# The router's chunks of a decoder step on two column halves of the array, and ranks counted in bfloat16

## The chip, the core and the metric

One core of a Trainium2 chip runs the whole program. It has a matrix engine (TensorE, in the profile PE, with its weight loads apart as PEld), a vector engine (VectorE, DVE), ScalarE (ACT), GpSimd (POOL) and a queue engine for transfers (SyncE, SP), all of them reading one on-chip memory (SBUF) of 128 partitions; TensorE writes to PSUM, eight banks of 512 f32 values in each partition. The metric is the time of one execution on the device, in microseconds; several executions are timed and their median is taken.

## The reference

One layer of a hybrid decoder over 1024 prompt rows and 8 sample rows, width 1024, all in f32. Two token mixers (sparse attention and a gated spatial one) give `merged`. What matters here comes behind them:

```
h = layer_norm(alpha * x + merged @ w_o, ln1_g, ln1_b)
lg = h @ w_router_group + b_router_group          # 4 groups
gsel = argmax(lg)
le = h @ w_router_expert[gsel] + b_router_expert  # 8 experts in each group
vals, eidx = top_k(le, 2)
weights = softmax(vals) * softmax(lg)[gsel]
f = sum over the two experts of  weight * (silu(h @ w_gate) * (h @ w_up)) @ w_down
y = layer_norm(alpha * h + f, ln2_g, ln2_b)
```

The kernel works only on the rows that chose an expert. So each row needs its two experts and, for each of them, its rank: how many rows ahead of it chose the same expert. The rank gives the row's place in the expert's list.

## The kernel before

The program runs through stages, each a block with an instruction list for every engine: projections and scores, choice of keys and gates, attention, then `merge_route_and_experts`, which the change touches. Engines signal one another by semaphores (`then_inc` and `wait_ge`); each list is worked off in the order in which it is written, and that order is set by hand.

**Merge.** 24 units, each the second branch's product of one block of 128 columns with a third of the rows (L1634 on TensorE), which VectorE multiplies with a gate and adds to (L1778, L1781). `gates` has three buffers. VectorE opens the block with a few clears (L1769 to L1772). Behind unit 16 (`FOLD_AT`) it folds the layer norm's gain into the router's weights, `w_fold` (L1786); TensorE later sums these over all rows (L1705).

**Projection and routing.** Nine tiles of 128 rows; the first has only 8 rows in use and is projected in another way (L1643). `project(i)` for i from 1 to 8 has 16 matmuls of 128x512 (two column halves c, eight chunks k, L1663), and between them stand the steps for the tile before, i - 1:

- ahead of matmul 2 (`TURN_AT`): `turn`, eight 128x128 transposes of h (L1675), which ScalarE copies to `hT` (L1754);
- ahead of 4 (`ROUTE_AT`): `route`, eight matmuls (L1685). The folded weights (128x36, a chunk of the width each) are stationary, `hT` (128x128) moves, and all eight add up to the logits of 4 groups and 32 experts, 36 partitions x 128 rows in PSUM;
- ScalarE copies these to `lgT` (L1759);
- ahead of 6 (`LOGITS_AT`): `turn_logits`, a transpose of `lgT` to 128 rows x 36 (L1691), which VectorE reads (L1900);
- VectorE chooses (`pick`): `both` is 1 where a row chose an expert, `chosen` the running count by row (L1818, L1824). Then it finishes h (L1930);
- ahead of 12 (`RANK_AT`): `rank`, two matmuls of 128x32 into one result: `earlier` (a triangle of ones) with `both` (L1699), and `ones` with `chosen` (L1700). VectorE turns the ranks into places (`place`, L1831 to L1847).

On VectorE the additions of the next tile (L1892, one for each column half) and their statistics (L1872) stand around `place`.

**Behind the ninth tile.** TensorE has `turn`, `route`, the sum of the first list of tokens (L1716), `turn_logits`, `rank`. VectorE makes `first_tokens` of that sum (L1869), GpSimd gathers these rows of h (L1970), and TensorE puts the first expert's rows together (L1724, L1731). The end of `route` also lets SyncE issue the load of the fourth expert's weights (L1582). Then come the 24 packs of the expert stage (L2087, L2100, L2119), whose weights have four buffers that are filled as the work goes on.

`ones` is f32, and so are `earlier`, `both` and `chosen`. `ident` is the 128x128 identity.

Of the kernel before, what the change touches and what calls it, by code (L numbers as in the profile page):

```python
# [12 lines left out]
F32 = mybir.dt.float32  # L13
BF16 = mybir.dt.bfloat16
# [6 lines left out]
P = 128  # L21
D = 1024
KC = D // P
# [3 lines left out]
TILES = NT + 1  # L27
# [1380 lines left out]
N_EXPERTS = 32  # L1408
# [10 lines left out]
SLOTS = TOK * N_EXPERTS  # L1419
NOWHERE = float(1 << 20)  # L1420
ROUTER = N_GROUPS + N_EXPERTS


def merge_route_and_experts(nc, ins, outs, keep, scratch):

    with nc.cleanup_on_exit(), ExitStack() as ctx:
        def sb(name, shape, dt=F32):
            return ctx.enter_context(nc.sbuf_tensor(name, shape, dt))
# [4 lines left out]
        ident, attnT, logits = keep["ident"], keep["attnT"], keep["router_logits"]  # L1433
        best_g, best1, best2 = (keep["best"][:, n, :] for n in range(3))
        chosen = keep["chosen"]
# [10 lines left out]
        w_fold = mergedT[:, :, SEQ + 32:SEQ + 32 + 2 * ROUTER].rearrange("p k (a r) -> p k a r", a=2)  # L1446
        h = keep["h_rows"]

        over = attnT[:].rearrange("p k n -> p (k n)")
        hT = over[:, 0:D].rearrange("p (k n) -> p k n", k=KC)  # L1450
# [12 lines left out]
        valid, away = sb("valid", [P, TILES]), sb("away", [P, TILES])  # L1463
        entry = sb("entry", [P, 2, TILES], U32)
        earlier = sb("earlier", [P, P])
        off_group = sb("off_group", [P, N_GROUPS])
        marked, rest, waste = (over[:, D + n * N_EXPERTS:D + (n + 1) * N_EXPERTS] for n in range(3))
        highest = sb("highest", [P, 1])
        lgT = over[0:ROUTER, D + 3 * N_EXPERTS:D + 3 * N_EXPERTS + P]
        FREE = D + 3 * N_EXPERTS + P  # L1470
        free = [over[:, FREE + n * N_EXPERTS:FREE + (n + 1) * N_EXPERTS] for n in range(10)]
        choice = [free[2 * n:2 * n + 2] for n in range(2)]
        both = free[4:6]
        after = FREE + 10 * N_EXPERTS + 2 * ROUTER
        e4 = over[:, after:after + TILES * N_GROUPS].rearrange("p (t g) -> p t g", g=N_GROUPS)
        e2, sum_g, den = (over[:, after + TILES * (N_GROUPS + n):after + TILES * (N_GROUPS + n + 1)] for n in range(3))
# [6 lines left out]
        ps = keep["ps"]  # L1483

        w_o_in, w_r_in, const_in = sem("w_o_in"), sem("w_r_in"), sem("m_const_in")
        fold_ready, folded, fold_read = sem("fold_ready"), sem("folded"), sem("fold_read")
# [18 lines left out]
        ranked = sem("ranked")  # L1505
# [122 lines left out]
        def _(pe):  # L1628
# [49 lines left out]
            def route(i):  # L1678
                pe.wait_ge(hT_read, 2 * i + 2)
                if i == 0:  # L1680
                    pe.wait_ge(fold_read, 2)
                else:
                    pe.wait_ge(logits_read, i)
                for k in range(KC):
                    mm = nc.tensor.matmul(ps[0:ROUTER, ROUTED, 0:P], w_fold[:, k, 0, :], hT[:, k, :],  # L1685
                                          start=(k == 0), stop=(k == KC - 1))
                mm.then_inc(routed, 1)

            def turn_logits(i):
                pe.wait_ge(lgT_read, i + 1)  # L1690
                nc.tensor.transpose(ps[:, ROUTED, P:P + ROUTER], lgT, ident[0:ROUTER, 0:ROUTER]).then_inc(lg_turned, 1)  # L1691

            def rank(i):

                pe.wait_ge(picked, i + 1)
                if i >= 1:
                    pe.wait_ge(slots_ready, i)
                to = ps[:, RANKS, 0:N_EXPERTS]
                nc.tensor.matmul(to, earlier[:], both[i % 2], start=True, stop=False)  # L1699
                nc.tensor.matmul(to, ones[:], chosen[:, i, :], start=False, stop=True).then_inc(ranked, 1)  # L1700

            pe.wait_ge(rows_zeroed, 1)
            pe.wait_ge(fold_ready, 2)
            for k in range(KC):
                mm = nc.tensor.matmul(ps[:, ROUTED, FOLD0:FOLD0 + 2 * ROUTER], ones[:],  # L1705
                                      w_fold[:, k, :, :].rearrange("p a r -> p (a r)"), start=(k == 0), stop=(k == KC - 1))
# [34 lines left out]
            rank(TILES - 1)  # L1741
            assemble_first()
            sum_tokens(1)
            nc.tensor.matmul(ps[:, TURNED[1], 0:N_EXPERTS], ones[:], chosen[:, TILES, :], start=True, stop=True).then_inc(counted, 1)
            main.tensor(pe)

        @block.scalar
        def _(act):
            for t in range(TILES):
                for c in range(2):  # L1750
                    act.wait_ge(h_turned, 2 * t + c + 1)
                    if t >= 1:
                        act.wait_ge(routed, t)
                    nc.scalar.copy(hT[:, c * 4:(c + 1) * 4, :],  # L1754
                                   ps[:, 6 + c, :].rearrange("p (k q) -> p k q", q=P)).then_inc(hT_read, 1)
                act.wait_ge(routed, t + 1)
                if t >= 1:
                    act.wait_ge(lg_turned, t)
                nc.scalar.copy(lgT, ps[0:ROUTER, 2, 0:P]).then_inc(lgT_read, 1)  # L1759
            main.scalar_first(act)  # L1760
            act.wait_ge(exp_ready, 2)
            nc.scalar.activation(e4, e4, ACT.Exp).then_inc(exped, 1)
            nc.scalar.activation(e2, e2, ACT.Exp).then_inc(exped, 1)
            main.scalar(act)

        @block.vector
        def _(dve):
            step = Chain(dve, dve_step)
            step(nc.vector.memset(chosen[:, 0, :], 0.0), wait=False)  # L1769
            step(nc.vector.memset(ones[:], 1.0), wait=False)  # L1770

            nc.vector.memset(mergedT[:, :, SEQ + N_SAMPLE:SEQ + FEW], 0.0).then_inc(rows_zeroed, 1)  # L1772
            for n, (blk, p) in enumerate(units):
                c0, width = PIECES[p]
                to = mergedT[:, blk, c0:c0 + width]
                dve.wait_ge(branch, n + 1)
                dve.wait_ge(gates_in[n % 3], 32 * (n // 3 + 1))
                nc.vector.tensor_tensor(to, ps[:, FIRST_BANK + n % 3, 0:width], gates[n % 3][:, 0, 0:width],  # L1778
                                        ALU.mult).then_inc(merged, 1)
                dve.wait_ge(merged, 2 * n + 1)  # L1780
                nc.vector.tensor_tensor(to, to, gates[n % 3][:, 1, 0:width], ALU.add).then_inc(merged, 1)  # L1781
                if n == FOLD_AT:
                    dve.wait_ge(w_r_in, 16)
                    dve.wait_ge(const_in, 16 * N_CONST)
                    for which in range(2):
                        nc.vector.tensor_tensor(w_fold[:, :, which, :], w_r[:],  # L1786
                                                ln1_t[:, which, :].unsqueeze(2).to_broadcast([P, KC, ROUTER]),
                                                ALU.mult).then_inc(fold_ready, 1)
            dve.wait_ge(folded, 1)
            nc.vector.tensor_scalar(minus_sum, ps[:, ROUTED, FOLD0:FOLD0 + ROUTER], -1.0, None, ALU.mult).then_inc(fold_read, 1)  # L1790
            nc.vector.tensor_tensor(b_r[:], b_r[:], ps[:, ROUTED, FOLD0 + ROUTER:FOLD0 + 2 * ROUTER], ALU.add).then_inc(fold_read, 1)
# [664 lines left out]
def build(nc, ins, outs, scratch):  # L2456
    with ExitStack() as whole:
        def sb(name, shape, dt=F32, side="left", ctx=whole):
            return ctx.enter_context(nc.sbuf_tensor(name, shape, dt, side=side))
# [35 lines left out]
        keep["w_gu_in"], keep["w_dn_in"] = ([whole.enter_context(nc.semaphore(f"{n}_expert{j}")) for j in range(W_BUFS)]  # L2495
                                            for n in ("w_gu_in", "w_dn_in"))
        for name, shape, dt in (("router_logits", [P, TILES, ROUTER], F32), ("weights", [P, 2, TILES], F32),
                                ("best", [P, 3, TILES], F32), ("chosen", [P, TILES + 1, N_EXPERTS], F32), ("ones", [P, P], F32),
                                ("h_rows", [P, TILES, D], F32), ("entries", [P, N_EXPERTS], U32), ("tokens", [P, N_EXPERTS], U32), ("most", [1, 1], I32)):
            keep[name] = sb(name, shape, dt)  # L2500
        keep["w_o"] = sb("w_o", [P, KC, D])
# [105 lines left out]
```

## Time and profile before

| | us |
|---|---|
| median of 3 runs | 1419.87 |
| the three runs | 1413.06, 1419.87, 1420.9 |
| span of the profiled execution | 1417.2 |
| PE busy | 1351.4 (95%) |
| PEld busy | 695.7 (49%) |
| DVE busy | 716.3 (51%) |
| ACT busy | 281.6 (20%) |
| POOL busy | 241.0 (17%) |
| DMA | 214.14 MB, mean 151 GB/s |

The profile is one execution, from its first to its last instruction. Times of its rows are counted from the span's start. The stage that the change touches lies between 845 and 1072 us. An f32 matmul shows as two records on PE and two on PEld, a transpose and a bfloat16 matmul as one. A row's duration covers the record's way through the array, so records that follow one another overlap; what one costs in a stream is the distance from its start to the next start. Numbers such as 128*36 in a row are rows and columns of the array in use.

### The profile page before, as it was taken

How to read it: one execution, taken by the hardware profiler on the slowest of the kernel's cores; microseconds unless marked ns; L12 is line 12 of the kernel's file. 1: busy time of each engine (PE TensorE's matmuls, PEld its weight loads, DVE VectorE, ACT ScalarE, POOL GpSimd, SP SyncE). 2: the span in 40 equal slices, each digit the busy share in tenths (PEclk: the TensorE clock that was granted, in tenths of full speed). 3: DMA queues.
4: the chain of work that ended last, by engine and by line, in shares of the span. 5: the costliest groups of instructions: out<-in, count | busy, mean ns of one | idle time of the engine just before them, and what ended most of it. 6: DMA issues, size and time to landing. Idle time of an engine off the chain costs nothing. (4 is left out here: it accounts for less than half of the span.)

```text
span 1417.2 us, 19227 instructions
## 1 busy us (share of the span) xinstructions
PE 1351.4 (95%) x6699; PEld 695.7 (49%) x6699; DVE 716.3 (51%) x1700; ACT 281.6 (20%) x624; POOL 241.0 (17%) x292
## 2 busy tenths in 40 slices
PE   8999999899999999999899989999988999999995
PEld 2444444344456666666577655555544333333321
DVE  0211123388888888997265853577782111111126
ACT  0100122232231111111266430000001111111115
POOL 3122000034330000011034400011111111111113
PEclk9999999999999999999899999999998999999998
DMA  9311002220022111110032319921135899999936
GB/s 323 94 51 60 17 16 75 76 65 0 0 101 73 68 67 67 67 67 31 26 101 66 127 43 332 366 103 30 30 102 231 329 399 410 405 408 413 407 140 259
DMA packets 70316, 214.14 MB, mean 151 GB/s; under 512 B 16059, under 2 KB 41915, under 8 KB 59866
## 3 DMA queue, kind: packets, MB, share of 16 engines
q1 hardware_dynamic: 56266, 184.74, 34.7%
q0 software_dynamic: 12688, 27.76, 5.8%
q8 instruction: 53, 0.87, 0.2%
q10 hardware_dynamic: 1280, 0.53, 0.2%
q14 instruction: 29, 0.24, 0.1%
HBM read 186.47 MB, written 34.65 MB: 156 GB/s over the span
## 5 line engine op out<-in xcount | busy, mean ns | idle before, releaser
L259 PE MATMUL ps_mixer<-front,x_all 128*128 128x512 f32 (+1 forms) x448 | 180.4, 557 | 1.7 <-ACT wi L407 1.7
L953 DVE TENSOR_SCALAR_CACHE_REDUCE front<-score,bound 128x384 bf16<-128x384 f32 (+2 forms) x198 | 174.0, 940 | 0.4 <-DVE bound L975 0.3
L259 PEld LDWEIGHTS ps_mixer<-front,x_all 128*128 128x128 f32 x448 | 83.2, 190 | 91.7 <-issue 81.2
L1663 PE MATMUL ps<-w_o,mergedT 128*128 128x512 f32 x256 | 117.7, 602 | 0.0
L2087 PE MATMUL ps<-w_gate_up,w_o 128*32 128x512 f32 (+1 forms) x640 | 113.2, 594 | 1.5 <-DVE w_o L2171 1.5
L781 PE MATMUL ps_mixer<-x_all,front 128*128 128x344 f32 x384 | 114.4, 453 | 0.0
L781 PE MATMUL ps_mixer<-x_all,w_gate 128*128 128x344 f32 x384 | 113.3, 453 | 0.0
L2087 PE MATMUL ps<-w_a,w_o 128*64 128x512 f32 (+1 forms) x256 | 113.1, 594 | 0.0
L2196 DVE TENSOR_TENSOR w_o<-w_o,ps 128x256 f32<-128x256 f32 x24 | 10.1, 420 | 164.0 <-ACT w_o L2151 164.0
L781 PEld LDWEIGHTS ps_mixer<-x_all,w_gate 128*128 128x128 f32 x384 | 72.7, 190 | 37.5
L781 PEld LDWEIGHTS ps_mixer<-x_all,front 128*128 128x128 f32 x384 | 72.6, 190 | 37.1
L953 DVE TENSOR_SCALAR_CACHE_REDUCE front<-score_s,bound 8x2049 bf16<-8x2049 f32 x33 | 77.0, 2334 | 0.0
L1663 PEld LDWEIGHTS ps<-w_o,mergedT 128*128 128x128 f32 x256 | 46.0, 190 | 48.2 <-issue 47.8
L2087 PEld LDWEIGHTS ps<-w_gate_up,w_o 128*32 128x32 f32 (+1 forms) x640 | 33.1, 115 | 68.8 <-issue 68.8
L935 POOL TENSOR_TENSOR front<-front 128x344 f32<-128x344 f32 x24 | 25.2, 1048 | 243.7 <-ACT front L895 243.7
L2065 POOL DMA_INDIRECT pair_out<-w_o,entries x24 | 25.0, 1042 | 236.1 <-DVE w_o L2203 236.1
L892 ACT ACTIVATE front<-ps_mixer,gate_bias 128x344 f32<-128x344 f32 x48 | 26.2, 547 | 175.8 <-PE ps_mixer L781 175.7
L1634 PE MATMUL ps<-attnT,w_a 128*128 128x344 f32 x186 | 56.0, 464 | 4.4 <-DVE mergedT L1778 2.9
L2119 PE MATMUL ps<-w_down,w_o 128*32 128x512 f32 (+1 forms) x320 | 60.0, 619 | 0.0
L2119 PE MATMUL ps<-gates,w_o 128*32 128x512 f32 (+1 forms) x128 | 58.1, 597 | 0.5 <-ACT w_o L2156 0.5
L729 PE MATMUL ps_mixer<-front,x_all 128*128 128x512 f32 x128 | 57.4, 592 | 0.0
L2087 PE MATMUL ps<-mergedT,w_o 128*32 128x512 f32 x384 | 56.5, 594 | 0.0
(342 smaller groups left out, 1933.6 us busy)
## 6 DMA issues: line engine op xcount, KB each, us to landing
w_gate_up<-in_w_gate_up SPq DMA_DIRECT2D x16, 2048.0 KB, 15.2
w_down<-in_w_down SPq DMA_DIRECT2D x16, 1024.0 KB, 16.6
w_a<-in_w_gate_up SPq DMA_DIRECT2D x8, 2048.0 KB, 11.7
mergedT<-in_w_gate_up SPq DMA_DIRECT2D x8, 2048.0 KB, 16.9
gates<-in_w_down SPq DMA_DIRECT2D x8, 1024.0 KB, 7.9
mergedT<-in_w_down SPq DMA_DIRECT2D x8, 1024.0 KB, 10.4
front<-in_w_qkvi SPq DMA_DIRECT2D x7, 930.0 KB, 16.7
w_gate<-in_w_gate SPq DMA_DIRECT2D x4, 1280.0 KB, 6.2
```

Of the source, the lines that this page charges most:

```text
L259: mm = nc.tensor.matmul(ps[:, g % 2, 0:c1 - c0], x_all[:, k, t * P:(t + 1) * P], w[:, k, c0:c1], start=(k == 0), stop=(k == KC - 1))
L729: mm = nc.tensor.matmul(ps[:, bank, :], x_all[:, k, t * P:(t + 1) * P], w_uv(k)[:, half * GW:(half + 1) * GW], start=(k == 0), stop=(k == ...
L781: mm = nc.tensor.matmul(ps[:, SETS[at % 2][which], 0:n], w_gate[j][:, which * KC + k, :], right[:, k, c0:c0 + n], start=(k == 0), stop=(k ...
L892: op = nc.scalar.activation(to, src, ACT.Sigmoid, bias=gate_bias[:, which, bass.ds(i * 2 + j, 1)])
L935: nc.gpsimd.tensor_tensor(m[:, 1, 0:n], m[:, 1, 0:n], m[:, 2, 0:n], ALU.mult).then_inc(multiplied, 1)
L953: V.tensor_scalar(waste[0:n, at - width:at], s, column(bound, g), None, compare, ALU.add, accum_out=column(number, g)).then_inc(taken, 1)
L1634: mm = nc.tensor.matmul(ps[:, FIRST_BANK + n % 3, 0:width], w_a[:, k, blk * P:(blk + 1) * P], attnT[:, k, c0:c0 + width], start=(k == 0), ...
L1663: mm = nc.tensor.matmul(ps[:, PROJECTED[i % 2][c], :], mergedT[:, k, t * P:(t + 1) * P], w_o[:, k, c * 512:(c + 1) * 512], start=(k == 0), ...
L2065: pool.indirect_dma_start(out=scratch["pair_out"].rearrange("t w q j d -> (t w q j) d"), out_offset=bass.IndirectOffsetOnAxis(ap=entries[: ...
L2087: mm = nc.tensor.matmul(ps[c0:c1, GU, :], rowsT[j][:, k, c0:c1], w_gu[b][:, k, :], start=(k == 0), stop=(k == KC - 1))
L2119: mm = nc.tensor.matmul(ps[c0:c1, 4 + 2 * j + c, :], hiddenT[j][:, k, c0:c1], w_dn[b][:, k, c * 512:(c + 1) * 512], start=(k == 0), stop=( ...
L2196: nc.vector.tensor_tensor(hidden[j], hidden[j], ps[:, GU, F:2 * F], ALU.mult).then_inc(hid, 1)
```

## The change

The router's even chunks go to the array's columns from 0 on, the odd ones to those from 64 on, and so to PSUM partitions 0 to 35 and 64 to 99: two sums of four chunks. ScalarE copies 100 partitions. The turn is no longer a transpose but an f32 matmul with `stack`, 100 rows x 36, which holds the identity in rows 0 to 35 and again in rows 64 to 99, so that it turns and adds the halves at once. Partitions between the halves are cleared once. For the ranks, `both` and `chosen` are written in bfloat16, `ones_b` and `earlier_b` are bfloat16 copies of the two stationary tiles, and the count of all rows (L1744) uses them too.

```diff
+LG_ROWS = P // 2 + ROUTER
...
+        earlier_b, ones_b = sb("earlier_b", [P, P], BF16), sb("ones_b", [P, P], BF16)
+        stack = sb("stack", [P, ROUTER])
...
-        lgT = over[0:ROUTER, D + 3 * N_EXPERTS:D + 3 * N_EXPERTS + P]
+        lgT = over[0:LG_ROWS, D + 3 * N_EXPERTS:D + 3 * N_EXPERTS + P]
...
-        both = free[4:6]
+        both = [free[4 + n].bitcast(BF16)[:, 0:N_EXPERTS] for n in range(2)]
...
                 for k in range(KC):
-                    mm = nc.tensor.matmul(ps[0:ROUTER, ROUTED, 0:P], w_fold[:, k, 0, :], hT[:, k, :],
-                                          start=(k == 0), stop=(k == KC - 1))
+                    half = k % 2 * (P // 2)
+                    mm = nc.tensor.matmul(ps[half:half + ROUTER, ROUTED, 0:P], w_fold[:, k, 0, :], hT[:, k, :],
+                                          start=(k < 2), stop=(k >= KC - 2))
...
-                nc.tensor.transpose(ps[:, ROUTED, P:P + ROUTER], lgT, ident[0:ROUTER, 0:ROUTER]).then_inc(lg_turned, 1)
+                nc.tensor.matmul(ps[:, ROUTED, P:P + ROUTER], lgT, stack[0:LG_ROWS, :], start=True, stop=True).then_inc(lg_turned, 1)
...
-                nc.tensor.matmul(to, earlier[:], both[i % 2], start=True, stop=False)
-                nc.tensor.matmul(to, ones[:], chosen[:, i, :], start=False, stop=True).then_inc(ranked, 1)
+                nc.tensor.matmul(to, earlier_b[:], both[i % 2], start=True, stop=False)
+                nc.tensor.matmul(to, ones_b[:], chosen[:, i, :], start=False, stop=True).then_inc(ranked, 1)
...
-            pe.wait_ge(fold_ready, 2)
+            pe.wait_ge(fold_ready, 3)
...
-                nc.scalar.copy(lgT, ps[0:ROUTER, 2, 0:P]).then_inc(lgT_read, 1)
+                nc.scalar.copy(lgT, ps[0:LG_ROWS, ROUTED, 0:P]).then_inc(lgT_read, 1)
...
+            step(nc.vector.memset(ones_b[:], 1.0), wait=False)
+            step(nc.vector.memset(ps[P // 4:P // 2, ROUTED, 0:P], 0.0), wait=False)
+            step(nc.vector.memset(stack[:], 0.0))
+            for q0 in (0, P // 2):
+                step(nc.vector.tensor_copy(stack[q0:q0 + ROUTER, :], ident[q0:q0 + ROUTER, q0:q0 + ROUTER]), wait=False)
...
+                    nc.vector.tensor_copy(earlier_b[:], earlier[:]).then_inc(fold_ready, 1)
...
-                                ("best", [P, 3, TILES], F32), ("chosen", [P, TILES + 1, N_EXPERTS], F32), ("ones", [P, P], F32),
+                                ("best", [P, 3, TILES], F32), ("chosen", [P, TILES + 1, N_EXPERTS], BF16), ("ones", [P, P], F32),
```

## Rows read from the trace of the kernel before

**Rows 1.** Stretches: bounds, length, busy by engine (x instructions), PEclk, DMA share, GB/s.

```profile
947.08:964.58 17.50, 17.50 (x63) 9.00 (x62) 12.88 (x45) 1.33 (x3) 2.66 (x4) 1.00 0.12 30
1066.00:1067.00 1.00, 1.00 (x7) 1.00 (x6) 0.85 (x3) 0.00 (x0) 0.00 (x0) 0.50 0.00 0
1143.00:1359.00 216.00, 216.00 (x1624) 73.46 (x1624) 32.43 (x54) 34.66 (x72) 34.45 (x34) 1.00 0.94 386
```

**Rows 2.** TensorE's timeline, one tile: start us, us, engine, line, out<-in, xcount.

```profile
947.08 1.04 PE L1675 MATMUL ps<-ident,h_rows 128*128 128x128 f32 x8
947.95 1.88 PE L1663 MATMUL ps<-w_o,mergedT 128*128 128x512 f32 x4
949.76 1.94 PE L1685 MATMUL ps<-attnT,mergedT 128*36 128x128 f32 x16
951.63 1.98 PE L1663 MATMUL ps<-w_o,mergedT 128*128 128x512 f32 x4
953.55 0.25 PE L1691 MATMUL ps<-ident,attnT 36*128 36x36 f32 x1
953.73 5.42 PE L1663 MATMUL ps<-w_o,mergedT 128*128 128x512 f32 x12
958.98 0.30 PE L1699 MATMUL ps<-attnT,earlier 128*128 128x32 f32 x2
959.12 0.39 PE L1700 MATMUL ps<-chosen,ones 128*128 128x32 f32 x2
959.34 5.40 PE L1663 MATMUL ps<-w_o,mergedT 128*128 128x512 f32 x12
```

**Rows 3.** The same tile on ScalarE and VectorE; in brackets idle time before.

```profile
951.74 0.26 ACT L1759 COPY attnT<-ps 36x128 f32<-36x128 f32 x1 [2.95 <-PE ps L1685]
...
953.91 0.25 DVE L1900 SCALAR_TENSOR_TENSOR attnT<-attnT,mv,ps 128x36 f32<-128x36 f32 x1 [3.40 <-PE ps L1691]
...
963.12 0.69 DVE L1892 SCALAR_TENSOR_TENSOR h_rows<-h_rows,ps 128x512 f32<-128x512 f32 x1
```

**Rows 4.** The timeline behind the ninth tile, VectorE, SyncE's queue and TensorE.

```profile
1053.90 1.28 DVE L1922 SCALAR_TENSOR_TENSOR h_rows<-h_rows,mv,ln 128x1024 f32<-128x1024 f32 x1
...
1054.77 0.33 SPq L1582 DMA_DIRECT2D mergedT<-in_w_gate_up  x1
...
1055.11 0.15 DVE L1869 TENSOR_SCALAR first_tokens<-ps 128x1 uint32<-128x1 f32 x1
...
1059.85 0.41 PE L1699 MATMUL ps<-attnT,earlier 128*128 128x32 f32 x2 [2.60 <-DVE attnT L1818]
...
1060.10 0.39 PE L1700 MATMUL ps<-chosen,ones 128*128 128x32 f32 x2
```

**Rows 5.** From the chain that ended last: start us, us, what.

```profile
1056.07 8.01 DMA w_o<-h,first_tokens
```

**Rows 6.** TensorE's timeline in the attention stage, two column halves of 64.

```profile
727.14 1.04 PE L1207 MATMUL ps<-ident,total 128*64 128x128 f32 x16
728.12 0.33 PE L1181 MATMUL ps<-ident,probs 128*128 128x128 f32 x1
```

**Rows 7.** TensorE's timeline, the single projection records ahead of turn and rank.

```profile
953.02 0.59 PE L1663 MATMUL ps<-w_o,mergedT 128*128 128x512 f32 x1
...
958.55 0.59 PE L1663 MATMUL ps<-w_o,mergedT 128*128 128x512 f32 x1
```

**Rows 8.** TensorE's timeline, bfloat16 matmuls among f32 ones in the gate stage.

```profile
651.91 0.55 PE L807 MATMUL ps_mixer<-ids_by_half,front 128*128 128x4 bf16 x16
652.32 4.87 PE L781 MATMUL ps_mixer<-x_all,front 128*128 128x344 f32 x16
```

**Rows 9.** VectorE's timeline, the first unit of the merge and the one after the fold.

```profile
847.97 0.52 DVE L1778 TENSOR_TENSOR mergedT<-ps,gates 128x344 f32<-128x344 f32 x1 [2.30 <-DMA gates<-merged_b]
...
891.65 0.52 DVE L1778 TENSOR_TENSOR mergedT<-ps,gates 128x344 f32<-128x344 f32 x1 [0.40 <-DMA gates<-merged_b]
```

**Rows 10.** The router's line: duration ns min/median/max, first and last start, forms.

```profile
L1685 PE MATMUL ps<-attnT,mergedT x144: 272/273/301, 914.8 to 1054.5; 128*36 128x128 f32 x144
```

More of the change, by code:

```diff
@@ L1743, in _ @@
             sum_tokens(1)
-            nc.tensor.matmul(ps[:, TURNED[1], 0:N_EXPERTS], ones[:], chosen[:, TILES, :], start=True, stop=True).then_inc(counted, 1)
+            nc.tensor.matmul(ps[:, TURNED[1], 0:N_EXPERTS], ones_b[:], chosen[:, TILES, :], start=True, stop=True).then_inc(counted, 1)
             main.tensor(pe)
```

## Prediction

> **What bounds the kernel now.** I read the table of stretches first, then the chain of waits, then the timelines of single engines inside one tile. In a tile of the routed projection TensorE is busy for all 17.50 us at full granted clock, with DMA at a share of 0.12 [rows 1]: TensorE's instruction order sets the pace, and each microsecond taken out of it is a microsecond of the span as long as no other engine becomes the last one. The 17.50 us are: eight transposes 0.87, four projection records 1.81, the router's 16 records 1.87 (949.76 to 951.63), four projection records 1.92, the turn of the logits 0.18, twelve records 5.25, the rank's four records 0.36 (958.98 to 959.34), twelve records 5.24 [rows 2]. An f32 matmul leaves two records, an f32 transpose one. The change touches only the 1.87, the 0.18 and the 0.36. Eight such tiles stand one behind the other, and the ninth's router stands in the tail.
>
> VectorE waits once in a tile, 3.40 us for the turned logits; from there (953.91) it works without a gap to the second half of the next addition (963.12) [rows 3]. Behind the ninth tile the chain leaves TensorE: VectorE runs to the first token list (1055.11) [rows 4], then a gather of 8.01 us holds everything [rows 5]. The expert stage is TensorE again, 216.00 us of 216.00 busy, with DMA at 0.94 beside it [rows 1].
>
> **The router on two column halves.** Removed: eight matmuls one after the other, 16 records at 1.87 / 16 = 0.117 us. Added: the same 16 records, alternating between columns 0 and 64 of the array. The nearest row has the same shape (128x128 moving, 64-column tiles, two halves alternating, also 16 records): L1207 starts at 727.14 and the next group at 728.12, so 0.98 us, 0.061 a record [rows 6]. Saved: 1.87 - 0.98 = 0.89 a tile. Ends: 0.053 a record (a 512-wide f32 record takes 0.43 [rows 7], a quarter of it is 0.107, and half of that) gives 1.02 saved; no overlap at all gives nothing. I take 0.89, because that row agrees in shape, type, count and order.
>
> The Trainium skill speaks against this. Its page "TensorE: Matmul & The Clock Gate" (Part 3, The mechanism) says that weight loads overlap matmuls in flight only when the row group differs, and both halves here use all rows. By it the halves would gain nothing and the sum would be that of rival A; the 0.061 of L1207, where the row groups don't differ either, disagrees.
>
> **The turn of the logits.** Removed: a transpose of one record on 36 rows. It costs 0.18 itself, and the projection record ahead of it lasts 953.55 - 953.02 = 0.53, against 0.43 for the record ahead of the rank (958.55 to 958.98) [rows 2, 7]: 0.10 more, paid where the array goes from 128 rows to 36. Together 0.28. Added: an f32 matmul with 100 rows and 36 columns moving, two records. The nearest is the rank's first matmul (128 rows, 32 moving), two records in 0.14 with its first weight load hidden [rows 2]. 100 rows need the whole array, so the 0.10 should go too. I take 0.14, saving 0.14. The other end: nothing hidden, 0.25 as in the tail (1059.85 to 1060.10) [rows 4], and still the 0.10: a loss of 0.07 a tile. For VectorE the second record comes about 0.03 later, so its wait ends 0.07 earlier, not 0.14.
>
> The Trainium skill, "TensorEngine Tiling (Array Packing)", Tiling Modes, says that a change of tiling mode drains the engine and a change of tile doesn't. The trace agrees in both parts (0.53 against 0.43, and L1207's cheap alternation). Were the 0.10 no drain but kept, the sum would be 0.7 us smaller.
>
> **The rank in bfloat16.** Removed: four f32 records, 0.36. Added: two bf16 records. Row: 16 bf16 records of L807 from 651.91 to 652.32, 0.026 each, among f32 matmuls and with no pause ahead of them [rows 8]. Two make 0.05; saved 0.31. The other end is half of the present price, 0.18 saved. I take 0.31, since L807 has the same 128x128 bf16 weights. Values are zeros, ones and counts to nine.
>
> **What is hidden.** At the block's start VectorE gets two more clears, one of a PSUM quadrant, one of the stack, and two 36-column copies: five small instructions. At 0.25 each, what L1900 takes on 36 columns [rows 3], that is 1.3 us; the first product waits 2.30 us for its gates anyway [rows 9]. Queued behind them are the zeroing of the merged rows, whose signal TensorE needs only after all 24 units, and nothing else early. The cast of the triangle comes behind unit 16, ahead of a wait of 0.40 [rows 9]; a product of 344 columns takes 0.52 [rows 9], so some 0.2 for 128 columns is my estimate and fits; if not, it delays one product by a few tenths, with three buffers of slack ahead of TensorE. No DMA is added or moved. ScalarE copies 100 partitions in place of 36; its copy (0.26) ends at 952.00, the turn begins at 953.55 [rows 2, 3], so even at five times the time it would be covered. VectorE writes its choices in bf16 with the same number of instructions; twelve projection records cover them, as now. If the cover of the start were gone it would be 1.3 us.
>
> **Who is late next.** A tile becomes 17.50 - 0.89 - 0.14 - 0.31 = 16.16 us. VectorE's loop: from the first transpose (947.08) to the start of L1900 (953.91) 6.83, after the change 6.83 - 0.89 - 0.07 = 5.87; then 9.21 without a gap to L1892 and its 0.69 [rows 2, 3]: 15.77. Only the second four transposes wait for it, 0.43 into their group, so with a signal of under 0.1 VectorE allows a tile each 15.4 us. TensorE at 16.16 stays the last, with some 0.7 to spare.
>
> **The sum.** The tail hangs on VectorE from the eighth turn (tile 7) on, so what counts is how much earlier that one comes: eight routers 8 x 0.89 = 7.12; seven turns 7 x 0.14 and the eighth's 0.07, 1.05; seven ranks 7 x 0.31 = 2.17. Together 10.34 us. The ninth tile's own router isn't last: the first token list follows VectorE's L1922 directly (1053.90 + 1.28, then 1055.11 [rows 4]). But its end releases the fourth expert's weights (issue at 1054.77), which share the DMA engines with the gather of 8.01 us [rows 4, 5]. They start 0.89 earlier against the gather: between 0 and 0.89 back, I take 0.5. Sum 10.8 us. The profiled execution's span is 1417.2 and becomes 1406.4. The median of the runs, 1419.87, is 2.7 above the span, with the same work around it: **1409.0 us**. With the other ends of turn and rank it is 7.12 - 0.49 + 1.26 = 7.9, 1412.0; with the best ends 8 x 1.02 + 1.05 + 2.17 + 0.89 = 12.3, 1407.6. The three runs before spread over 7.8 us, so a median is good to about 3.
>
> **Rivals.**
> A. The halves don't overlap: a record on one half waits for the other's, 0.117 each as now. Left are turn and rank, 3.2 us: **1416.7**. For it only that this kernel's router tiles are 36 wide, not 64; against it L1207. Chance 0.07.
> B. The front gain is given back behind the ninth tile. TensorE ran the assembly there at a granted clock of 0.50 (1.2 of 2.4 GHz), after it had idled for the gather [rows 1]. With less work around the idle time it may fall earlier or rise later and take the first expert products along: 7 us of these at half clock would cost 7. The expert stage's DMA share of 0.94 also leaves gathers little room, so that a changed meeting with a weight load may cost 1 to 4. Against: no transfer there runs by its own clock; the loads are released by TensorE's progress and move along. I price it at 3.5 lost: **1412.5**. Chance 0.16.
> C. Slower: each change of half drains. A record lasts 0.273 [rows 10]; if each of the router's eight changes waited for that, it would take 16 x 0.117 + 8 x 0.273 = 4.06, 2.19 more, less 0.45 for turn and rank: 1.74 a tile, 14 us, **1434**. It decides from a price of 0.17 a change (0.98 + 8 x 0.17 = 1.87 + 0.45). The drain seen is 0.10, at changes of mode only. Chance 0.03.
> D. The change is compiled to something else (a 36-column tile placed at 64 taking the whole array, say): within 0.3% of before. Chance 0.04, near **1418**.
>
> **How the numbers follow.** Forecast 0.70 at 1409.0, its own range 1406 to 1413. The range for 8 in 10 reaches to B and to the edge of A: 1405 to 1417. Over or under 0.5%, about what a measurement of this kernel can tell from no change, means under 1412.8: nine tenths of the forecast's 0.70 and half of B, 0.71. Slower by 0.5% is C and chance, 0.04. The rest, 0.25, is A, D, half of B and the edge of the forecast.
>
> **What would show it.** Right: the router's 16 records in 0.95 to 1.0 us; the projection record ahead of the turn at 0.43; two bf16 records in under 0.1; a tile period near 16.2; VectorE's wait at L1900 down from 3.40 to about 2.1; first token list some 10 us earlier than 1055.11; an expert stage of the same length. Wrong: router records still at 0.117 (A), or longer (C); a period at 15.4 or above 16.5 with TensorE waiting for VectorE's additions; an assembly and first expert that take 3 us more (B).

## The result and the profile after

| | before | after |
|---|---|---|
| median of the runs timed together, us | 1419.05 (4 runs) | 1406.53 (4 runs, 1406.22 to 1408.59) |
| ratio after / before, 95% | | 0.9916, 0.9896 to 0.9936 |
| span of the profiled execution, us | 1417.2 | 1407.2 |
| one tile of the routed projection, us | 17.50 | 16.17 |
| router / turn / rank on TensorE, us | 1.87 / 0.18 / 0.36 | 1.00 / 0.14 / 0.06 |
| first token list written, us | 1055.11 | 1045.37 |

Timed once more with six runs, the changed kernel came to 1405.24 us, ratio 0.9912 (0.9896 to 0.9927). It is 0.8 to 0.9% faster.

The table of stretches of the changed kernel, with the columns of [rows 1]: a tile, and the expert stage.

```profile
945.00:961.17 16.17, 16.17 (x61) 7.90 (x60) 12.88 (x45) 1.34 (x3) 2.66 (x4) 1.00 0.13 33
1142.00:1347.00 205.00, 205.00 (x1546) 69.82 (x1538) 30.68 (x51) 32.73 (x68) 32.42 (x32) 1.00 0.95 388
```

TensorE is still busy for the whole tile, and VectorE has the same 12.88 us of work in it as before. TensorE's order sets the pace as it did; the tile is simply 1.33 us shorter. The expert stage looks as it did in [rows 1].

TensorE's timeline of that tile, which answers to [rows 2]:

```profile
945.00 1.04 PE L1678 MATMUL ps<-ident,h_rows 128*128 128x128 f32 x8
945.87 1.88 PE L1666 MATMUL ps<-w_o,mergedT 128*128 128x512 f32 x4
947.69 1.07 PE L1689 MATMUL ps<-attnT,mergedT 128*36 128x128 f32 x16
948.69 1.98 PE L1666 MATMUL ps<-w_o,mergedT 128*128 128x512 f32 x4
950.51 0.31 PE L1695 MATMUL ps<-stack,attnT 100*128 100x36 f32 x2
950.65 5.40 PE L1666 MATMUL ps<-w_o,mergedT 128*128 128x512 f32 x12
955.88 0.18 PE L1703 MATMUL ps<-attnT,earlier_b 128*128 128x32 bf16 x1
955.91 0.18 PE L1704 MATMUL ps<-chosen,ones_b 128*128 128x32 bf16 x1
955.94 5.40 PE L1666 MATMUL ps<-w_o,mergedT 128*128 128x512 f32 x12
```

As before, the differences of starts are what one reads, not the durations, since pipelined records overlap. The router's 16 records take 948.69 - 947.69 = 1.00 us, the turn's two 0.14, the rank's two 0.06. The weight loads of the same stretch show two more things:

```profile
947.68 0.81 PEld L1689 LDWEIGHTS ps<-attnT,mergedT 128*36 128x36 f32 x16 [0.76 <-issue]
...
950.08 0.19 PEld L1695 LDWEIGHTS ps<-stack,attnT 100*128 100x128 f32 x1 [0.24 <-issue]
```

The first load of the turn runs at 950.08, under the last projection record, which takes 0.43 us (950.08 to 950.51) where [rows 7] had 0.53. The router's first load does not run ahead: it starts at 947.68, together with its matmul (947.69). The four projection records in front of it take 1.82 us (945.87 to 947.69) in place of four times 0.43, so about 0.10 us is paid there, as it was before the change.

ScalarE and VectorE of the tile, with idle time before in brackets, which answers to [rows 3]; the last row is VectorE's first product of the merge, which answers to [rows 9]:

```profile
948.80 0.27 ACT L1763 COPY attnT<-ps 100x128 f32<-100x128 f32 x1 [2.09 <-PE ps L1689]
...
950.94 0.25 DVE L1909 SCALAR_TENSOR_TENSOR attnT<-attnT,mv,ps 128x36 f32<-128x36 f32 x1 [2.07 <-PE ps L1695]
...
960.14 0.69 DVE L1901 SCALAR_TENSOR_TENSOR h_rows<-h_rows,ps 128x512 f32<-128x512 f32 x1
```

```profile
848.63 0.52 DVE L1786 TENSOR_TENSOR mergedT<-ps,gates 128x344 f32<-128x344 f32 x1 [1.32 <-DMA gates<-merged_b]
```

VectorE's wait fell from 3.40 to 2.07 us, and the 9.20 us behind it (950.94 to 960.14) are the old 9.21. At the front, the first product still waits for its gates, 1.32 us where it was 2.30: the new small instructions took 0.98 us out of a wait.

SyncE's issue of the fourth expert's weights and VectorE's first token list, then the chain that ended last behind the ninth tile, which answer to [rows 4, 5]:

```profile
1044.17 0.33 SPq L1585 DMA_DIRECT2D mergedT<-in_w_gate_up  x1
...
1045.37 0.15 DVE L1878 TENSOR_SCALAR first_tokens<-ps 128x1 uint32<-128x1 f32 x1
```

```profile
1046.33 7.77 DMA w_o<-h,first_tokens
1054.24 3.75 PE ps L1728 x16
...
1064.42 2.30 DMA list_of<-entry,slot_out
...
1069.99 11.94 DMA w_o<-h,tokens
...
1083.07 5.27 PE ps L2128 x32
```

The chain is the old one. The gather of the first token rows takes 7.77 us where it took 8.01.

To compare runs I cut every profiled execution at the same events. The columns, in us: the merge stage's first gates load (a time); from there to the first record of the few-row projection; on to VectorE's read of the eighth turned logits; on to the issue of the first token gather; on to the first expert product; on to the transposes of the third pack; on to those of the fourth; on to the end.

```
                       start   few  8th read gather product pack3 pack4    end    span
before                845.16 60.55   135.70  14.66  15.88  19.94 13.66 311.65  1417.2
after                 845.75 60.54   125.49  14.55  15.76  19.88 13.67 311.56  1407.2
after_again           844.90 60.41   125.49  14.55  14.84  19.99 11.96 310.56  1402.7
e1_halves_only        847.50 59.76   127.67  14.56  14.43  20.18 11.97 310.23  1406.3
e2_ranks_only         845.45 62.75   133.52  14.54  15.88  20.01 13.60 311.45  1417.2
e3_turn_only          845.32 58.86   134.60  14.56  16.46  20.10 11.97 310.63  1412.5
e4_halves_in_blocks   845.94 61.25   129.20  14.54  14.42  19.61 13.60 311.54  1410.1
e9_halves_in_pairs    848.70 62.56   125.70  14.56  14.03  19.52 13.60 311.63  1410.3
e6_late_load          845.66 60.80   125.49  14.55  12.67  21.46 11.96 311.41  1404.0
e7_early_list         844.49 60.25   125.49  14.55  14.81  19.49 11.97 310.45  1401.5
e8_both               847.98 62.40   125.49  14.55  12.88  18.81 13.47 310.82  1406.4
e10_early_list_calm   845.39 59.85   125.49  14.55  15.08  16.10 11.97 311.57  1400.0
e11_.._late_loads     849.52 62.33   125.50  14.54  12.89  16.10 11.97 311.75  1404.6
```

(In the last row the label is shortened: e11_early_list_late_loads.) Between before and after, the column of the eighth read gives 10.21 us, and all others together 0.2 the other way. In that column programs with the same instructions agree to 0.01 us, while the first two columns scatter by 5 and 4 us. That is why the terms are judged in it, not by the medians.

### The profile page after: what moved, and what is told of

The parts are those of the page before. It is cut to its first block and busy times, and to the rows that moved or that the text cites. A ratio compares the mean times of both kernels' runs of the same rounds, so it can differ in the third digit from the quotient of the medians.

```text
span 1407.2 us, 19213 instructions
## 1 busy us (share of the span) xinstructions
PE 1339.1 (95%) x6689; PEld 684.7 (49%) x6689; DVE 717.5 (51%) x1706; ACT 281.8 (20%) x624; POOL 241.4 (17%) x292
```

## Experiments

### The three edits apart

**The halves without the bfloat16 ranks** (e1). The rank goes back to f32, the rest stays:

```diff
-                nc.tensor.matmul(to, earlier_b[:], both[i % 2], start=True, stop=False)
-                nc.tensor.matmul(to, ones_b[:], chosen[:, i, :], start=False, stop=True).then_inc(ranked, 1)
+                nc.tensor.matmul(to, earlier[:], both[i % 2], start=True, stop=False)
+                nc.tensor.matmul(to, ones[:], chosen[:, i, :], start=False, stop=True).then_inc(ranked, 1)
```

> The halves and the stacked turn, with the ranks back in f32 (no bfloat16 copies). Theory (three separate costs on TensorE's list): router 16 records in 1.00 us as in the changed kernel, turn 0.14, rank back at 0.36 from 0.06, so a tile period of 16.17 + 0.30 = 16.47 us and 8 us gained against before, 1411. Rival (the bfloat16 writes also relieve VectorE, and that is part of the gain): the period is longer than 16.47.

Measured: 1409.13 us (ratio 0.9937, 0.9918 to 0.9956). TensorE's timeline at the rank:

```profile
957.48 0.30 PE L1702 MATMUL ps<-attnT,earlier 128*128 128x32 f32 x2
...
957.84 5.40 PE L1665 MATMUL ps<-w_o,mergedT 128*128 128x512 f32 x12
```

The rank is back at 0.36, router and turn stay at 1.00 and 0.14, and the eighth read comes 2.18 us later than in the changed kernel.

**The ranks alone** (e2): the kernel before with `earlier_b`, `ones_b`, `both` and `chosen` in bfloat16 and nothing else.

> The kernel before with the ranks in bfloat16 alone. Theory: period 17.50 - 0.30 = 17.20 us, 7 to 8 times 0.30 = 2.2 us gained, which timing alone can hardly tell from nothing. Rival (a bfloat16 matmul among f32 ones costs a switch): rank over 0.10 us and a period above 17.3.

Measured: 1417.39 us (0.9994, 0.9976 to 1.0011). TensorE's timeline at the rank:

```profile
960.86 0.18 PE L1700 MATMUL ps<-attnT,earlier_b 128*128 128x32 bf16 x1
960.88 0.18 PE L1701 MATMUL ps<-chosen,ones_b 128*128 128x32 bf16 x1
960.91 5.40 PE L1664 MATMUL ps<-w_o,mergedT 128*128 128x512 f32 x12
```

0.05 us instead of 0.36, and the eighth read 2.18 us earlier than before: seven ranks of 0.31, the same from both sides. By the medians alone, a change of 2 us can't be seen here.

**The turn alone** (e3): ranks in f32, and all eight chunks of the router on columns 0 to 35 again. The stacked turn stays, and the PSUM tile is cleared whole, so that rows 64 to 99 add zeros.

```diff
-                    half = k % 2 * (P // 2)
+                    half = 0
                     mm = nc.tensor.matmul(ps[half:half + ROUTER, ROUTED, 0:P], w_fold[:, k, 0, :], hT[:, k, :],
-                                          start=(k < 2), stop=(k >= KC - 2))
+                                          start=(k == 0), stop=(k == KC - 1))
```

> Ranks in f32, all eight router chunks on columns 0 to 35 as before, but the turn by the 100-row matmul with the stack (the second half is zeros). Theory (the 0.10 ahead of the turn is the price of going from 128 rows to 36): the projection record ahead of the turn lasts 0.43 in place of 0.53, the turn 0.14, router still 1.87, period 17.50 - 0.14 = 17.36, and 1 us gained. Rival (the 0.10 is the price of the wait on the copy, which stays here): 0.53 ahead of the turn and a period of 17.46 or more.

Measured: 1416.71 us (0.9996, 0.9977 to 1.0014). TensorE's timeline:

```profile
947.93 1.94 PE L1688 MATMUL ps<-attnT,mergedT 128*36 128x128 f32 x16
949.80 1.98 PE L1665 MATMUL ps<-w_o,mergedT 128*128 128x512 f32 x4
951.62 0.31 PE L1694 MATMUL ps<-stack,attnT 100*128 100x36 f32 x2
951.76 5.40 PE L1665 MATMUL ps<-w_o,mergedT 128*128 128x512 f32 x12
```

The router is at 1.87 again, so the columns alone make its gain. The four projection records ahead of the turn take 1.82 us (949.80 to 951.62) where they took 1.92, and the turn takes 0.14: 0.14 a tile, and the eighth read is 1.10 us earlier. The 0.10 thus belonged to the 36-row tile, not to the wait in front of it, which is still there. Nor does a transpose as such cost it: in [rows 2] the twelve projection records ahead of the 128-row transposes take 5.24 us (959.34 to 964.58, the end of the tile in [rows 1]), those ahead of the rank 5.25. It goes with what the Trainium skill says in "TensorEngine Tiling (Array Packing)", Tiling Modes, that a change of mode drains the array and a change of tile does not: the 100-row tile needs the whole array, as its neighbours do.

The three parts add up: 2.18 for the ranks, 1.10 for the turn, and 10.21 - 2.18 - 1.10 = 6.93 for the halves, which is 8 x 0.867.

### How the halves overlap

**Chunks 0 to 3 on the first half, 4 to 7 on the second** (e4): one change of half in place of seven.

```diff
-                    half = k % 2 * (P // 2)
+                    half = k // (KC // 2) * (P // 2)
                     mm = nc.tensor.matmul(ps[half:half + ROUTER, ROUTED, 0:P], w_fold[:, k, 0, :], hT[:, k, :],
-                                          start=(k < 2), stop=(k >= KC - 2))
+                                          start=(k % (KC // 2) == 0), stop=(k % (KC // 2) == KC // 2 - 1))
```

> The changed kernel with chunks 0 to 3 on the first half and 4 to 7 on the second, in this order, so the half changes once in a router and not at each chunk. Theory (two halves overlap only where matmuls of both stand next to each other in the list): nearly no overlap, 16 records in 1.87 - 0.06 to 1.87, period 17.0 us, 1413. Rival 1 (shorter sums or 64-column weights are what makes it fast): 1.00 and 16.17 as with alternation. Rival 2 (the array looks ahead through its list far enough to run both halves at once): also near 1.0.

Measured: 1411.42 us (0.9945, 0.9925 to 0.9965). TensorE's timeline:

```profile
949.51 1.53 PE L1689 MATMUL ps<-attnT,mergedT 128*36 128x128 f32 x16
950.98 1.98 PE L1666 MATMUL ps<-w_o,mergedT 128*128 128x512 f32 x4
```

A miss. I had thought that only records that follow each other overlap, so that a block order would cost as much as one half. The router takes 1.47 us, 0.40 less than one half does, and the eighth read comes 3.71 us after that of the alternating order: 8 x 0.46. The starts of the single records in the trace show where the 0.40 comes from. The first five start at 949.51, 949.65, 949.76, 949.87 and 949.98, the 0.11 apart that one half needs. Then a second series begins, at 949.98, 950.12, 950.23 and so on, while the first goes on at 950.08, 950.19 and 950.30. The trace doesn't name a record's half; but each series keeps the 0.11 of one half, so the second can only be the other half, started while three of the first half's eight records were still to start. TensorE looked ahead in its list past these three and took a matmul out of the order in which they were written.

**A change of half every second chunk** (e9):

```diff
-                    half = k % 2 * (P // 2)
+                    half = k // 2 % 2 * (P // 2)
                     mm = nc.tensor.matmul(ps[half:half + ROUTER, ROUTED, 0:P], w_fold[:, k, 0, :], hT[:, k, :],
-                                          start=(k < 2), stop=(k >= KC - 2))
+                                          start=(k in (0, 2)), stop=(k in (5, 7)))
```

> The changed kernel with the half changed at each second chunk (0, 1 on the first, 2, 3 on the second and so on). With alternation the 16 records take 1.00 us, in blocks of four chunks they took 1.47, where 1.87 was the price in one half. Theory, formed after the blocks (a matmul starts as soon as its own half is free, as far as some four records ahead): pairs are four records, so close to full overlap, 1.0 to 1.1 us. Rival (only direct neighbours overlap, one matmul at each change): the blocks saved 0.40 at one change, pairs have three and would save at most what alternation does, but end at 1.2 or more.

TensorE's timeline:

```profile
952.71 1.10 PE L1689 MATMUL ps<-attnT,mergedT 128*36 128x128 f32 x16
953.74 1.98 PE L1666 MATMUL ps<-w_o,mergedT 128*128 128x512 f32 x4
```

1.03 us, and 125.70 against 125.49 for the eighth read. Here two records start 0.01 us apart from the first pair on (952.709 and 952.722), although three more of the first half stand between them in the list. Four records in a row on one half are bridged almost fully, eight aren't. The reading of e4 holds, and the rival that asked for 1.2 us or more falls. The one time of this kernel, 1412.08 us, says nothing on it: the stage ahead began 3 us late and took 2 us longer (848.70 and 62.56 in the table).

### What limits the tile next

**Much less work on TensorE** (e5): the router takes only chunks 0 and 1, and the projection leaves out chunks 3 and 5.

```diff
+                        if k in (3, 5):
+                            continue
...
-                for k in range(KC):
+                for k in (0, 1):
...
-                                          start=(k < 2), stop=(k >= KC - 2))
+                                          start=True, stop=True)
```

> The changed kernel with part of TensorE's work left out, so its outputs are not the reference's: the router adds only chunks 0 and 1 of 8, and each projection half leaves out chunks 3 and 5 of 8. It asks how far VectorE is from being the last in a tile. TensorE's own list would take 16.17 - 0.75 - 8 x 0.43 = 12.0 us a tile. Theory (VectorE's run of 9.9 us without a gap, then second half of the transposes, two projections, router, one projection, turn and read): 9.9 + 0.05 + 0.43 + 1.82 + 0.25 + 0.96 + 0.40 = 13.8 us a tile, with TensorE waiting for VectorE's second addition. Rival (VectorE is no limit as long as its busy share is under 0.8): 12.0.

TensorE's timeline, with what ended its idle time, and VectorE's behind the turned logits:

```profile
951.35 0.19 PE L1705 MATMUL ps<-attnT,earlier_b 128*128 128x32 bf16 x1 [0.82 <-DVE attnT L1829]
...
957.10 0.66 PE L1680 MATMUL ps<-ident,h_rows 128*128 128x128 f32 x4 [0.72 <-DVE h_rows L1903]
...
965.36 0.19 PE L1705 MATMUL ps<-attnT,earlier_b 128*128 128x32 bf16 x1 [0.82 <-DVE attnT L1829]
```

```profile
961.16 0.25 DVE L1911 SCALAR_TENSOR_TENSOR attnT<-attnT,mv,ps 128x36 f32<-128x36 f32 x1
...
970.37 0.69 DVE L1903 SCALAR_TENSOR_TENSOR h_rows<-h_rows,ps 128x512 f32<-128x512 f32 x1
```

The tile takes 14.01 us (951.35 to 965.36), 0.2 above the theory's and 2.0 above the rival's time. (The single run's 1394.59 us isn't compared: with work left out, other rows go to the experts.) TensorE now waits twice in it, 0.72 for VectorE's addition ahead of the second four transposes and 0.82 for the picks ahead of the rank; the second wait was in no expectation. VectorE goes from the turned logits to its addition in the same 9.21 us. So the loop through VectorE is real and as long as the forecast had it, and the changed kernel at 16.17 runs just above it.

### The meeting of loads and gathers behind the ninth tile

The forecast let the fourth expert's load move by 0.89 us against the gather of the first rows. How much that load costs the gather was a guess. Five kernels and the changed kernel again ask for it.

> The changed kernel once more, beside the kernel before and the two variants of this call, to hold their times against. Theory: 10 to 12 us under before.

Measured: 1405.24 us (0.9912, 0.9896 to 0.9927); the gather takes 7.42 us.

**The load behind the last store of h** (e6):

```diff
-                if i + 1 == TILES:
-                    sp.wait_ge(routed, TILES)
-                    sp.dma_start(keep["w_gate_up"][W_AHEAD][:], ins["w_gate_up"][W_AHEAD]).then_inc(keep["w_gu_in"][W_AHEAD], 16)
...
                                  ).then_inc(h_out if i + 1 < TILES else last_h_out, 16)
+            sp.wait_ge(routed, TILES)
+            sp.dma_start(keep["w_gate_up"][W_AHEAD][:], ins["w_gate_up"][W_AHEAD]).then_inc(keep["w_gu_in"][W_AHEAD], 16)
```

> The changed kernel with the fourth expert's weights (2 MB) issued behind the last store of h, no longer ahead of the gather of the first token list. Theory (the gather's 7.8 us are the load's, which shares the DMA engines): the gather takes some 4.6 us, the assembly starts 3 us earlier, and 3 to 5 us are gained against the changed kernel, as the weights are needed only by the third pack. Rival (the load's bytes must pass at some time, and now meet the expert stage's gathers): the gather is shorter, but the stall of TensorE ahead of the second pack's successor (3.0 us) grows by as much; no gain.

Measured: 1404.85 us (0.9901, 0.9887 to 0.9916). From the chain that ended last:

```profile
1046.50 4.45 DMA w_o<-h,first_tokens
...
1061.51 3.62 DMA list_of<-entry,slot_out
...
1068.30 12.29 DMA w_o<-h,tokens
```

The gather falls to 4.45 us, so the load costs it 3.0 to 3.3 by the two profiles of the changed kernel, and the first expert product comes 2.2 to 3.1 us earlier. But the scatter of the token list now meets the load, 3.62 for 2.30, and the third pack takes 21.46 for 19.88 to 19.99: half is given back.

**The last tile's list ahead of the second gather** (e7): GpSimd issues the last two scatters one step earlier.

```diff
+            for which in range(2):
+                scatter(TILES - 1, which)
             pool.wait_ge(first_ready, 2)
             pool.wait_ge(last_h_out, 32)
...
-            for which in range(2):
-                scatter(TILES - 1, which)
```

> The changed kernel with the last tile's two entries scattered on GpSimd ahead of the second first-token gather, in place of behind it. Theory (the list waits only for GpSimd's order): its choices are ready at 1054.3, so the list can be read some 6 us earlier, the gather of the third pack starts at about 1063 in place of 1070, TensorE's stall of 3.0 us before 1082 goes with the low clock after it: 3 to 5 us gained. Rival (the gather lands late because the DMA engines are full, whenever it is issued): no gain.

Measured: 1403.56 us (0.9895, 0.9874 to 0.9916). GpSimd's timeline, and from the chain:

```profile
1053.73 1.06 POOL L1605 DMA_INDIRECT list_of<-entry,slot_out  x1 [7.88 <-DVE slot_out L1856]
...
1059.26 1.07 POOL L1979 DMA_INDIRECT w_o<-h,first_tokens  x1 [3.19 <-DVE first_tokens L1878]
```

```profile
1059.26 9.12 DMA w_o<-h,first_tokens
...
1070.50 8.65 PE ps L2096 x32
```

The wait for the third pack is gone, and another stands in its place: the second gather of first rows, issued at 1059.26, takes 9.12 us among the loads that SyncE issued from 1057.62 on.

**Both** (e8).

> Both moves at once. Theory: the gains add up, 6 to 9 us under the changed kernel, near 1399. Rival: one of them takes the other's room, no more than the better of the two.

Measured: 1405.61 us (0.9908, 0.9891 to 0.9926). From the chain:

```profile
1060.73 6.04 DMA list_of<-entry,slot_out
```

The late load now falls on the scatter, 6.04 us for 2.30. Product (12.88) and third pack (18.81) come earlier than in the changed kernel, but together 2.7 us later than in e11 below, where the load meets neither gather nor scatter: the gains of e6 and e7 don't add.

**The early list with the next loads held back** (e10): as e7, and SyncE waits with the down weights of the fourth expert (index `W_BUFS - 1`, 3; the expectation calls them the third's) and the layer norm rows behind them until the second gather has landed.

```diff
-                sp.wait_ge(rows_in[0], 16)
+                sp.wait_ge(rows_in[1], 16)
                 load_down(W_BUFS - 1)
```

> The variant with the early list, and the third expert loads (1 MB of w_down and 1 MB of layer norm rows) wait for the second first-token gather, not the first. With the early list alone they were issued at 1057.6 to 1059.0, just ahead of that gather (1059.26), which took 9.1 us. Theory: the gather takes some 5 us again, the second pack's transposes don't wait, and 2 to 3 us are gained against the early list alone, near 1401. Rival (the loads now meet the next gather, of the third pack, and that becomes the last one): as the early list alone, 1403.6.

Measured: 1403.53 us (0.9894, 0.9877 to 0.9911). From the chain:

```profile
1060.36 7.07 PE ps L2096 x64
...
1069.44 7.09 PE ps L2096 x32
```

The third pack comes after 16.10 us in place of 19.9: the stall is gone and both groups of products run at full pace.

**The same with the fourth load moved to that point as well** (e11).

> As the calm early list, and the fourth expert's 2 MB are issued at the same late point, so that both first-token gathers have the DMA engines to themselves. Theory: the first gather 4.45 in place of 7.2 to 7.8 us, 3 us more, near 1398. Rival (3 MB of loads then meet the third and fourth pack's gathers, as in the variant with both moves, which ended at 1405.6): 1404 or more.

Measured: 1404.55 us (0.9894, 0.9877 to 0.991). The stretches from the gather on are the shortest of all, 12.89 and 16.10. Its profiled execution began the stage 4 us later than e10's (849.52) and took 62.33 to the few rows, for which no run gives a reason.

The times of these variants fell short of what was expected. Against the changed kernel's 1405.24, e6 was to gain 3 to 5 us and gained 0.4; e7 was to gain as much and gained 1.7; e8 was to end near 1399, e10 near 1401, e11 near 1398, and they ended at 1405.61, 1403.53 and 1404.55, as their rivals had it. The stretches show that the waits moved or went; the medians show little of it.

From the few rows to the fourth pack (the sum of five columns) the changed kernel takes 189.35 and 186.83 us in its two profiles, e10 183.19, e11 181.00: 4 to 8 us better. (1.7 us of the distance to the first profile is the clock in the last of these columns, see the last section.) By their medians they are 1 to 3 us better, with intervals that overlap. Both beat the kernel before, by 1.06%; that they beat the changed one isn't shown.

## Why the prediction held, point by point

- **TensorE's order sets the pace.** Right: 16.17 us of 16.17 busy, for a forecast period of 16.16.
- **Router.** 0.87 a tile for the 0.89 taken from L1207 [rows 6]: 6.93 for 7.12. The row of the same shape, type, count and order was the right one to trust. Rival A falls: both halves use all 128 rows, and their records overlap, 1.00 us for 16 against 1.87 on one half in e3. With it falls, for this case, the sentence of the Trainium skill that the forecast set against itself ("TensorE: Matmul & The Clock Gate", Part 3, The mechanism), that weight loads overlap matmuls in flight only when the row group differs. That the halves would then gain nothing was more than the page says: the same Part 3 lists a measured speedup of 2.38 for three tiles packed by columns. Rival C falls too, as no change of half cost anything.
- **Turn.** 0.14 and the 0.10 of drain gone: 1.10 for 1.05 in the sum. e3 shows it by itself.
- **Rank.** 0.31 a tile, 2.18 for 2.17, from both sides in e1 and e2.
- **Hidden work.** The forecast named two clears and two copies and counted five; it is three clears (`ones_b` as well) and two copies, and they took 0.98 us for the 1.3 allowed. The merge's first product still waits 1.32 us for its gates; ScalarE's copy of 100 partitions takes 0.27 for 0.26. VectorE's wait fell to 2.07, forecast about 2.1.
- **Who is late next.** The VectorE loop lies under 16.17, shown with e5. Whether its limit is the 15.4 of the forecast was tested only at 14, where it was 0.2 off.
- **Load against gather.** 0.5 us taken. The two main profiles give 0.24 (8.01 to 7.77) and the second of the changed kernel 0.59 (7.42), but one pair can't size this term. The load was issued 2.16 us ahead of the gather's start (1044.17 to 1046.33) where it had been 1.30, as forecast. Six profiles have the 2.16 (e9 2.14): 7.77, 7.42, e1 7.18, e9 7.18, e7 7.18, e10 6.89, on average 7.27. Three have 1.3: 8.01, e2 8.28, e3 8.13, on average 8.14. That is 0.87, near the upper end of the forecast's 0 to 0.89, and e4 lies between with 1.70 and 7.59. What the forecast didn't see is how much is there: the meeting costs 2.4 to 3.3 us in these six (against 4.45 in e6). In e8 and e11, which move the load too, TensorE starts its assembly 4.47 and 4.53 us behind the gather's issue, in e6 4.58.
- **Rival B** (the gain given back behind the ninth tile) didn't come: product 15.76 for 15.88, third pack 19.88 for 19.94, fourth 13.67 for 13.66. Its mechanisms are real, though: loads and gathers cost each other microseconds in e6 to e8, and the clock does fall there (below).
- **The sum.** 10.3 us earlier at the first token list: 1055.11 - 1045.37 = 9.74, with the stage begun 0.59 later. The profiled spans differ by 10.0. The medians differ by 12.5 and, in the second comparison, 13.4, with intervals of 9.1 to 14.8 and 10.4 to 14.8 us. The 10.21 of the stretch and the 0.87 of the gather's average are 11.1, inside both. The 1.4 to 2.3 us above it aren't located, and with such intervals need not be there. By the ratios of the variants nothing of the kind shows: e1 8.9 us for 8.0 + 0.87 by the trace, e2 0.9 for 2.2, e3 0.6 for 1.1. One thing of this size is on record, the place where the clock falls (last section), worth 1.7 us; how often each kernel has it in which place wasn't counted. The two medians lie 2.5 and 3.8 us under the forecast's 1409.0; the second is also just under its own range of 1406 to 1413, and inside 1405 to 1417.

## What to carry to other kernels

Where one engine is busy for the whole of a repeated tile, price the edit from differences of starts in rows of the same shape, type and order, and multiply only up to the last tile that the following chain hangs on; here this came out within 0.2 us in 10. In this kernel matmuls with weights of at most 64 columns gain from alternating between column halves even if both use all rows: for 128 moving columns (36 and 64 columns of weights) and for 512 (a pair of the expert stage's 128*64 records takes 0.43 us, as one record of the full width does). Four records in a row on one half cost next to nothing (1.03 for 1.00 us), eight cost half of the gain. And where medians scatter by more than the edit, cut each trace at the same events and compare the stretches: an edit of 1 us can be read to 0.05 that way, while the medians say only that nothing happened.

## What the hardware showed that I had not expected

**TensorE looks ahead in its list.** 16 records in 1.00 us alternating, 1.03 in pairs of chunks, 1.47 in blocks of four chunks, 1.87 on one half; in the blocks, the other half's first matmul starts while three records ahead of it in the list haven't.

**A small gather beside a 2 MB load.** 4.45 us without the load, 6.9 to 7.8 with it issued 2.2 us ahead, 8.0 to 8.3 with 1.3 us ahead; the scatter of a token list 2.30 us in the changed kernel and 6.04 with the load issued 4 us ahead of it. Moving the load mostly moved the price; of the places tried, only that of e11 left both short.

**The clock falls after the stalls, at one of two places, in the same program.** Stretches of the changed kernel and of its second profile, with the columns of [rows 1]:

```profile
1083.00:1085.00 2.00, 2.00 (x13) 0.55 (x16) 0.69 (x1) 0.25 (x1) 0.00 (x0) 0.62 0.99 426
```

```profile
1081.20:1083.20 2.00, 2.00 (x21) 0.67 (x24) 0.69 (x1) 0.27 (x2) 0.00 (x0) 1.00 0.86 336
```

A stretch of the second profile somewhat earlier, and TensorE's timeline there:

```profile
1071.00:1073.00 2.00, 2.00 (x6) 0.60 (x4) 0.00 (x0) 0.00 (x0) 0.00 (x0) 0.50 0.98 352
```

```profile
1070.57 0.95 PE L2096 MATMUL ps<-w_gate_up,w_o 128*64 128x512 f32 x1 [0.36 <-DVE w_o L2180]
...
1071.32 1.06 PE L2096 MATMUL ps<-w_gate_up,w_o 128*64 128x512 f32 x1
```

In the first, the down products behind the wait for the pack gather take 5.27 us; in two of these the granted clock is 0.62 on average, so it changes between its two levels (1.2 and 2.4 GHz) within them. In the second they run at the full clock and take 3.57, but the gate and up products ahead of that wait ran at half the clock, a pair each 0.85 us for 0.43, and the wait for the gather hid it. The fourth pack thus follows after 13.67 or 11.96 us with not one instruction changed. Of the thirteen profiles in the table five show 13.6 to 13.7, seven 11.96 to 11.97, and e8 13.47. In e10, where the wait is gone, the clock falls at neither place. What decides between the two I did not find.
